# A fast matrix product over seven instead of six k pairs, with its recombination in one place

## The chip, the cores and the metric

One Trainium2 chip, one NeuronCore. The metric is the time on the device in microseconds (us), median of three runs. TensorE multiplies (its records are PE, and PEld for the loading of its stationary operand), VectorE (DVE) and ScalarE (ACT) work on vectors, GpSimd (POOL) issues some DMAs, SyncE (SP) issues the loads of the weights.

## The reference, cut to what matters

A decoder layer on 256 tokens of width 4096: attention in four branches, then a layer that retrieves experts. Its last step is the product that the change touches:

```
coef = gates * take_along_axis(act, experts)
wmat = zeros((256, 4096)).at[rows, experts].add(coef)      # float32
h = h + wmat @ v                                          # v is 4096 x 4096, float32
```

## The kernel before

**Products of float32.** TensorE multiplies a reduced form of float32 (fp32r). For full accuracy the kernel splits each operand in a high part (hi, rounded by ScalarE) and a remainder (lo = raw - hi, by VectorE), and computes hi x hi + lo x hi + hi x lo: three matmuls of 128 x 128 by 128 x 512 for each block product.

**Chunks and the ring.** Weights come in chunks of two k tiles by 512 columns (512 KB, 128 x 1024 floats) into a ring of four slots. For each chunk: SyncE loads `w_raw`, ScalarE makes `w_hi` (`hi`, L1091), VectorE makes `w_lo` (`lo`, L1484), TensorE multiplies. ScalarE may overwrite a slot of `w_hi` when TensorE has used the chunk four before (`chunk_used`), so the conversions run up to three chunks ahead of TensorE. SyncE loads into a slot of `w_raw` as soon as VectorE has made its `w_lo`.

**The V product.** Rows of wmat are two halves h of 128 tokens, columns of v are eight groups of 512, k is 32 tiles of 128, taken as 16 k pairs. Groups 0 and 1 run plainly. Groups 2 to 7 run as three column pairs m = 1, 2, 3 (`for m in range(1, PAIRS)`, each engine has this loop, L1077, L1469, L2195). One step of it is one k pair: two chunks, s for the pair's first column group and s + 1 for its second. Both hold the same two k tiles. In a plain k pair that is two halves x two k tiles x two groups = 8 block products, 24 matmuls. `products` (L582) does one chunk, 12 matmuls. The text calls the two column groups of a column pair block 0 and block 1, and numbers chunks from the start of column pair 1, 32 to each.

**The fast k pairs** (`FAST`, L93: 0, 2, 4, 6, 8, 10) treat these as 2 x 2 matrices of blocks and use Winograd's form of Strassen's method: 7 block products, 21 matmuls (`fast_products`, L993). It needs sums of the left blocks (`s_raw`, `s_hi`, `s_lo`, made once for all fast k pairs, in the last chunks of group 1: L2081, L1461, L2096) and sums of the right blocks per k pair: VectorE's `t_sums` (L2102) makes four blocks t, ScalarE `t_hi` (L1446), VectorE `t_lo` (L2120). t is held once: t_sums waits for the t_lo of the fast k pair before, t_hi for TensorE's last use of t (`t_used`). Four of the seven products are summed over all fast k pairs in the four banks of `side` (P1, P5, P6, P7), the others directly in the four banks of `acc`, one for each block and half, where the plain k pairs add too.

**The recombination** (`add_pure`, L2139): once per column pair VectorE adds P1, P1 + P6, P1 + P6 + P5 and so on into the rows of h, in nine instructions of 512 columns in four steps; behind five of them (L2147, L2149, L2150, L2154, L2158) VectorE waits for their own end through `then`, before the next may start. The last raises `pure_free`; TensorE waits for it before it starts the side banks of the next column pair (L1033). Before, steps 0 and 1 lie around the second conversion of k pair 13, steps 2 and 3 around that of k pair 14.

**The block additions** (`end_of_pair`, `add_block`, L2162): VectorE adds the `acc` banks of the column pair before to the rows of h, and each raises `block_free`. They stand in k pair 1 of the next column pair: both halves of block 0, then the conversion of chunk 34, then both halves of block 1, then that of chunk 35. TensorE waits for each bank before its first matmul into it (`wait_block`): in k pair 0, after P1's two hi matmuls and the nine matmuls from t, for block 0's first half, two matmuls later for block 1's, and before its last three for block 0's second half; in k pair 1 for block 1's second half.

**VectorE's order at the seam** between column pairs is its program's: conversions of k pair 15 (chunks 30 and 31), t_sums for the next column pair's k pair 0, conversions of chunk 32 and half of 33, t_lo, and then k pair 1 as above.

Of the kernel before, what the change touches and what calls it, by code (L numbers as in the profile page):

```python
# [69 lines left out]
CPG = KT // 2  # L70
# [19 lines left out]

CH_F = CH_V + 2 * CPG
PAIRS = GRP // 2
FAST = (0, 2, 4, 6, 8, 10)  # L93
NF = len(FAST)

NCMP = (S - 32) // 16 + 1
# [73 lines left out]
def fast_count(m, kp):  # L170

    return (m - 1) * NF + FAST.index(kp)

# [9 lines left out]
def build(nc, io):  # L183
# [175 lines left out]
    def sems(*names):  # L359
        return [nc.alloc_semaphore(n) for n in names]  # L360
# [41 lines left out]
    half_done, pure_free, block_free, last_stored = sems("half_done", "pure_free", "block_free", "last_stored")  # L402
# [20 lines left out]
    def pair_bank(i):  # L423

        return (GN_V + i) % 2
# [58 lines left out]
    with nc.Block() as block:  # L484
# [96 lines left out]
        def _(pe):  # L581
# [401 lines left out]
            def ring(slot):  # L983
                return [[w[:, slot, j * 512:(j + 1) * 512] for j in range(2)] for w in (w_hi, w_lo)]
# [8 lines left out]
            def fast_products(m, kp):  # L993

                n, a = fast_count(m, kp), CH_F + (m - 1) * 2 * CPG + 2 * kp
                first, last = kp == FAST[0], kp == FAST[-1]
                wa, wb = ring(a % RING), ring((a + 1) % RING)
                q = FAST.index(kp)
                s_tile = [(s_hi[:, i, q, :], s_lo[:, i, q, :]) for i in range(4)]
# [77 lines left out]
            for m in range(1, PAIRS):  # L1077
                for kp in range(CPG):
                    if kp in FAST:
                        fast_products(m, kp)  # L1080
# [5 lines left out]
        def _(act):  # L1086
# [4 lines left out]
            def hi(chunk, slot, width, m4):  # L1091

                act.wait_ge(raw_loaded[slot], raw_parts(m4) * 16)
                if not (isinstance(chunk, int) and chunk < RING):
                    act.wait_ge(chunk_used, chunk - (RING - 1))
                nc.scalar.activation(w_hi[:, slot, 0:width], w_raw[:, slot, 0:width], ACT.Copy).then_inc(hi_ready, 1)  # L1096
# [358 lines left out]
            def hi_half(chunk, slot):  # L1455

                act.wait_ge(raw_loaded[slot], raw_parts(chunk // RING) * 16)
                act.wait_ge(chunk_used, chunk - (RING - 1))
                nc.scalar.activation(w_hi[:, slot, 512:1024], w_raw[:, slot, 512:1024], ACT.Copy).then_inc(hi_ready, 1)
# [9 lines left out]
            for m in range(1, PAIRS):  # L1469
                for kp in range(CPG):  # L1470
                    s = CH_F + (m - 1) * 2 * CPG + 2 * kp
                    hi(s, s % RING, 1024, s // RING)
                    if kp in FAST:
                        hi_half(s + 1, (s + 1) % RING)
# [6 lines left out]
        def _(dve):  # L1481
            then = chain(dve, dve_chain)

            def lo(chunk, slot, width):  # L1484
                dve.wait_ge(hi_ready, chunk + 1)
                nc.vector.tensor_tensor(w_lo[:, slot, 0:width], w_raw[:, slot, 0:width],  # L1486
                                        w_hi[:, slot, 0:width].bitcast(F32), ALU.subtract).then_inc(lo_ready, 1)
# [306 lines left out]
            def add_rows(g, ch0, parity, rows=rows):  # L1794

                dve.wait_ge(chunk_used, g * CPG + (ch0 + CPG))
                for h in range(NT):
                    dst = rows[:, h, bass.ds(g * 512, 512)]
                    e = nc.vector.tensor_tensor(dst, acc[:, parity, h, :], dst, ALU.add)
                e.then_inc(bank_free[parity], 1)  # L1800
# [301 lines left out]
            def t_sums(m, kp):  # L2102

                n, s = fast_count(m, kp), CH_F + (m - 1) * 2 * CPG + 2 * kp
                a = s % RING
                if n == 0:
                    dve.wait_ge(s_lo_done, 4)
                else:
                    dve.wait_ge(t_lo_done, 2 * n)
                for i in range(2):  # L2110
                    dve.wait_ge(raw_loaded[a + i], raw_parts(s // RING) * 16)
                nc.vector.tensor_tensor(
                    t_raw[:, 0], w_raw[:, a + 1, :].rearrange("p (j n) -> p j n", j=2), w_raw[:, a:a + 2, 0:512],
                    ALU.subtract).then_inc(t_made, 1)
                dve.wait_ge(t_made, 2 * n + 1)
                then(nc.vector.tensor_tensor(t_raw[:, 1, 0], w_raw[:, a + 1, 512:1024], t_raw[:, 0, 0], ALU.subtract))
                nc.vector.tensor_tensor(t_raw[:, 1, 1], w_raw[:, a, 512:1024], t_raw[:, 1, 0], ALU.subtract)\
                    .then_inc(t_made, 1)

            def t_lo_part(m, kp):  # L2120

                n = fast_count(m, kp)
                for d in range(2):
                    dve.wait_ge(t_hi_done, 2 * n + d + 1)
                    nc.vector.tensor_tensor(flat(t_lo[:, d]), flat(t_raw[:, d]), flat(t_hi[:, d]).bitcast(F32),  # L2125
                                            ALU.subtract).then_inc(t_lo_done, 1)

            def lo_half(chunk, slot):

                dve.wait_ge(hi_ready, chunk + 1)  # L2130
                nc.vector.tensor_tensor(w_lo[:, slot, 512:1024], w_raw[:, slot, 512:1024],
                                        w_hi[:, slot, 512:1024].bitcast(F32), ALU.subtract).then_inc(lo_ready, 1)

            def block_rows_of(m, i, h):

                n = 2 * m + i
                return h_rows[:, h, n * 512:(n + 1) * 512]

            def add_pure(m, step):  # L2139

                u, v = sums[0][:], sums[1][:]
                p1, p5, p6, p7 = (side[:, i, :] for i in range(4))
                if step == 0:
                    dve.wait_ge(t_used, m * NF)
                    c = block_rows_of(m, 0, 0)
                    nc.vector.tensor_tensor(c, p1, c, ALU.add)
                    then(nc.vector.tensor_copy(u, p1))  # L2147
                elif step == 1:
                    then(nc.vector.tensor_tensor(u, p6, u, ALU.add))  # L2149
                    then(nc.vector.tensor_tensor(v, p5, u, ALU.add))  # L2150
                elif step == 2:
                    c = block_rows_of(m, 1, 0)
                    nc.vector.tensor_tensor(c, c, v, ALU.add)
                    then(nc.vector.tensor_tensor(u, p7, u, ALU.add))  # L2154
                else:
                    c = block_rows_of(m, 0, 1)
                    nc.vector.tensor_tensor(c, c, u, ALU.add)
                    then(nc.vector.tensor_tensor(v, p5, u, ALU.add))  # L2158
                    c = block_rows_of(m, 1, 1)
                    nc.vector.tensor_tensor(c, c, v, ALU.add).then_inc(pure_free, 1)  # L2160

            def add_block(m, i, h):  # L2162

                s = CH_F + m * 2 * CPG - 2 + i
                if h == 0:
                    dve.wait_ge(half_done, 2 * (m - 1) + i + 1)
                else:
                    dve.wait_ge(chunk_used, s + 1)
                c = block_rows_of(m, i, h)
                nc.vector.tensor_tensor(c, acc[:, pair_bank(i), h, :], c, ALU.add).then_inc(block_free, 1)  # L2170

            def end_of_pair(m, i):

                if m == 0:
                    if i == 1:
                        add_rows(1, CH_V, pair_bank(1), h_rows)
                else:
                    for h in range(NT):
                        add_block(m, i, h)

# [14 lines left out]
            for m in range(1, PAIRS):  # L2195
                for kp in range(CPG):
                    s = CH_F + (m - 1) * 2 * CPG + 2 * kp
                    if kp == 1:
                        end_of_pair(m - 1, 0)
                    lo(s, s % RING, 1024)  # L2200
                    if kp in FAST:
                        lo_half(s + 1, (s + 1) % RING)
                        t_lo_part(m, kp)
                        continue
                    if kp == 1:
                        end_of_pair(m - 1, 1)
                    if kp in (13, 14):
                        add_pure(m, 2 * (kp - 13))
                    lo(s + 1, (s + 1) % RING, 1024)
                    if kp + 1 in FAST:  # L2210
                        t_sums(m, kp + 1)
                    elif kp == CPG - 1 and m + 1 < PAIRS:
                        t_sums(m + 1, 0)
                    if kp in (13, 14):
                        add_pure(m, 2 * (kp - 13) + 1)
            for i in range(2):
                end_of_pair(PAIRS - 1, i)

# [152 lines left out]
```

## Time and profile before

| | |
|---|---|
| median of 3 runs | 1919.16 us (1918.83 to 1919.18) |
| profiled execution | 1918.33 us, span 1916.5 us |
| TensorE matmuls busy | 1912.1 us, 9230 instructions |
| VectorE busy | 1369.7 us (71%) |
| ScalarE busy | 962.2 us (50%) |
| granted clock | 1.000 |
| DMA | 412.70 MB, 215 GB/s |

Busy time is the union of an engine's instructions. Matmuls overlap in the records (the next starts before the one before it is recorded as ended), so a busy TensorE is one without gaps, and the distance between starts is what a matmul costs.

### The profile page before, as it was taken

The numbers are of one execution on the slowest core, as the hardware profiler recorded it, in microseconds if no ns is written. First come the engines' busy times: TensorE is split into PE (matmuls) and PEld (weight loads), VectorE is DVE, ScalarE is ACT, GpSimd is POOL, SyncE is SP. The second block draws the span as 40 slices with busy tenths as digits, with TensorE's granted clock in tenths as the row PEclk, the third lists the DMA queues.
The fourth block names the chain that finished last, engine by engine and source line by source line (L and its number), as shares of the span: only waits on it lengthen the run. The fifth ranks groups of instructions, "written<-read, shape, count | busy, mean of one in ns | idle before, by whom it ended". The sixth has DMA issues, their size and how long they took to land.

```text
span 1916.5 us, 26452 instructions
## 1 busy us (share of the span) xinstructions
PE 1912.1 (100%) x9230; PEld 1577.6 (82%) x9230; DVE 1369.7 (71%) x1999; ACT 962.2 (50%) x1184; POOL 36.3 (2%) x49
## 2 busy tenths in 40 slices
PE   9999999999999999999999999999999999999999
PEld 8888888888888888888888888888887788888887
DVE  6578775575557889655555555788879877789796
ACT  7653644445566556444444464444444454555453
POOL 0010010000000000000000000000000000000000
PEclk9999999999999999999999999999999999999999
DMA  9976667556655669877777776677766668666664
GB/s 324 352 221 166 168 176 195 170 156 168 182 183 176 185 194 295 290 225 239 236 229 236 215 227 221 229 213 216 218 210 190 186 200 306 209 215 212 206 221 152
DMA packets 198688, 412.70 MB, mean 215 GB/s; under 512 B 45776, under 2 KB 123984, under 8 KB 197936
## 3 DMA queue, kind: packets, MB, share of 16 engines
q1 hardware_dynamic: 173904, 369.35, 63.6%
q10 hardware_dynamic: 20976, 25.19, 3.9%
q0 software_dynamic: 3696, 16.65, 2.3%
q8 instruction: 73, 1.20, 0.3%
q14 instruction: 39, 0.32, 0.0%
HBM read 390.15 MB, written 20.97 MB: 215 GB/s over the span
## 4 chain that ended last, share of the span: by engine, by line
PE 100%; DVE 0%; issue 0%
PE acc L590 27%; PE acc L593 27%; PE acc L597 27%; PE acc L638 3%; PE acc L640 3%; PE acc L644 3%; PE acc L1066 1%; PE side L768 1%; PE side L979 1%; PE side L980 1%; PE side L981 1%; PE side L879 1%; PE acc L613 1%; PE acc L609 1%; PE acc L617 1%; PE acc L1071 0%
## 5 line engine op out<-in xcount | busy, mean ns | idle before, releaser
L1486 DVE TENSOR_TENSOR w_lo<-w_raw,w_hi 128x1024 fp32r<-128x1024 f32 (+1 forms) x662 | 802.9, 1215 | 496.7 <-ACT w_hi L1096 493.7
L1096 ACT ACTIVATE w_hi<-w_raw 128x1024 fp32r<-128x1024 f32 (+1 forms) x662 | 695.6, 1052 | 757.8 <-PE acc L597 655.3
L590 PE MATMUL acc<-w_hi,xt_hi 128*128 128x512 f32 x1484 | 402.0, 393 | 0.0
L593 PE MATMUL acc<-w_hi,xt_lo 128*128 128x512 f32 x1484 | 397.0, 389 | 0.0
L597 PE MATMUL acc<-w_lo,xt_hi 128*128 128x512 f32 x1484 | 396.9, 389 | 0.0
L593 PEld LDWEIGHTS acc<-w_hi,xt_lo 128*128 128x128 f32 x1484 | 278.6, 188 | 58.6
L597 PEld LDWEIGHTS acc<-w_lo,xt_hi 128*128 128x128 f32 x1484 | 278.6, 188 | 58.2
L590 PEld LDWEIGHTS acc<-w_hi,xt_hi 128*128 128x128 f32 x1484 | 275.7, 188 | 56.7 <-issue 1.8
L590 PE MATMUL acc<-w_hi,x_hi 128*128 128x512 f32 x640 | 175.1, 395 | 0.0
L593 PE MATMUL acc<-w_hi,x_lo 128*128 128x512 f32 x640 | 171.8, 390 | 0.0
L597 PE MATMUL acc<-w_lo,x_hi 128*128 128x512 f32 x640 | 171.2, 389 | 0.0
L593 PEld LDWEIGHTS acc<-w_hi,x_lo 128*128 128x128 f32 x640 | 120.1, 188 | 25.7
L597 PEld LDWEIGHTS acc<-w_lo,x_hi 128*128 128x128 f32 x640 | 120.2, 188 | 25.3
L590 PEld LDWEIGHTS acc<-w_hi,x_hi 128*128 128x128 f32 x640 | 117.2, 188 | 22.4
L1238 ACT ACTIVATE gate<-acc 128x512 f32<-128x512 f32 x64 | 34.8, 596 | 37.1 <-PE acc L597 35.5
L1453 ACT ACTIVATE t_hi<-t_raw 128x1024 fp32r<-128x1024 f32 x36 | 36.1, 1051 | 15.7 <-PE acc L981 15.7
L2125 DVE TENSOR_TENSOR t_lo<-t_raw,t_hi 128x1024 fp32r<-128x1024 f32 x36 | 42.4, 1219 | 0.8 <-ACT t_hi L1453 0.8
L590 PE MATMUL acc<-w_hi,zt_hi 128*128 128x512 f32 x128 | 34.5, 391 | 0.0
L597 PE MATMUL acc<-w_lo,zt_hi 128*128 128x512 f32 x128 | 34.2, 389 | 0.0
L593 PE MATMUL acc<-w_hi,zt_lo 128*128 128x512 f32 x128 | 34.2, 389 | 0.0
L1731 DVE TENSOR_TENSOR gate<-acc,gate 128x512 f32<-128x512 f32 x48 | 30.7, 682 | 0.0
L1180 ACT ACTIVATE probs<-probs,small 128x128 f32<-128x128 f32 (+2 forms) x44 | 18.3, 417 | 22.0 <-DVE small L1644 21.9
(330 smaller groups left out, 1756.7 us busy)
## 6 DMA issues: line engine op xcount, KB each, us to landing
w_raw<-in_stream SPq DMA_DIRECT2D x504, 512.0 KB, 4.2
w_raw<-in_w_in SPq DMA_DIRECT2D x16, 496.0 KB, 3.9
w_raw<-in_w_in SPq DMA_DIRECT2D x16, 480.0 KB, 4.1
w_raw<-in_w_in SPq DMA_DIRECT2D x16, 464.0 KB, 3.7
w_raw<-in_w_in SPq DMA_DIRECT2D x16, 448.0 KB, 3.9
w_raw<-in_w_in SPq DMA_DIRECT2D x16, 432.0 KB, 3.8
w_raw<-in_w_in SPq DMA_DIRECT2D x16, 416.0 KB, 4.1
w_raw<-in_w_in SPq DMA_DIRECT2D x16, 400.0 KB, 3.7
```

The lines of the kernel that those rows point to most:

```text
L590: pe.matmul(o[h], lhs(k0 + j, h)[0], wh[j], start=first and j == 0, stop=False)
L593: pe.matmul(o[h], lhs(k0 + j, h)[1], wh[j], start=False, stop=False)
L597: mm = pe.matmul(o[h], lhs(k0 + j, h)[0], wl[j], start=False, stop=last and j == 1)
L638: pe.matmul(o, lhs(k0 + j, h)[0], wh[j], start=first and j == 0, stop=False)
L640: pe.matmul(o, lhs(k0 + j, h)[1], wh[j], start=False, stop=False)
L644: mm = pe.matmul(o, lhs(k0 + j, h)[0], wl[j], start=False, stop=last and j == 1)
L1096: nc.scalar.activation(w_hi[:, slot, 0:width], w_raw[:, slot, 0:width], ACT.Copy).then_inc(hi_ready, 1)
L1238: e = nc.scalar.activation(gate[:, n % 2, h, :], acc[:, 1, h, :], ACT.Sigmoid)
L1453: nc.scalar.activation(flat(t_hi[:, d]), flat(t_raw[:, d]), ACT.Copy).then_inc(t_hi_done, 1)
L1486: nc.vector.tensor_tensor(w_lo[:, slot, 0:width], w_raw[:, slot, 0:width], w_hi[:, slot, 0:width].bitcast(F32), ALU.subtract).then_inc(lo_ ...
L1731: nc.vector.tensor_tensor(dst, acc[:, 0, h, :], gate[:, n % 2, h, :], ALU.mult)\
L2125: nc.vector.tensor_tensor(flat(t_lo[:, d]), flat(t_raw[:, d]), flat(t_hi[:, d]).bitcast(F32), ALU.subtract).then_inc(t_lo_done, 1)
```

## The change

The list of fast k pairs gets k pair 12. All four steps of the recombination move to k pair 15: two ahead of the conversion of its second chunk, two behind it, and ahead of t_sums for the next column pair. The block additions get a wait for `pure_free`. The S tiles grow with the list (`NF` is 7).

```diff
-FAST = (0, 2, 4, 6, 8, 10)
+FAST = (0, 2, 4, 6, 8, 10, 12)
 NF = len(FAST)
...
                 else:
+                    dve.wait_ge(pure_free, m)
                     for h in range(NT):
                         add_block(m, i, h)
...
                     if kp == 1:
                         end_of_pair(m - 1, 1)
-                    if kp in (13, 14):
-                        add_pure(m, 2 * (kp - 13))
+                    if kp == CPG - 1:
+                        add_pure(m, 0)
+                        add_pure(m, 1)
                     lo(s + 1, (s + 1) % RING, 1024)
+                    if kp == CPG - 1:
+                        add_pure(m, 2)
+                        add_pure(m, 3)
                     if kp + 1 in FAST:
                         t_sums(m, kp + 1)
                     elif kp == CPG - 1 and m + 1 < PAIRS:
                         t_sums(m + 1, 0)
-                    if kp in (13, 14):
-                        add_pure(m, 2 * (kp - 13) + 1)
```

## Rows read from the trace of the kernel before

**Rows 1.** The chain that ended last, share of the span by engine.
```profile
PE 100%; DVE 0%; issue 0%
```

**Rows 2.** Busy time by stage: stretch, length, each engine's busy us, PEclk, DMA share, GB/s.
```profile
1747.30:1830.30 83.00, 83.00 (x368) 68.73 (x367) 71.17 (x76) 42.58 (x44) 1.43 (x2) 1.00 0.67 215
1742.00:1754.00 12.00, 12.00 (x54) 9.93 (x54) 11.61 (x14) 7.27 (x9) 1.43 (x2) 1.00 0.72 243
1825.00:1837.00 12.00, 12.00 (x54) 9.95 (x53) 11.61 (x14) 7.32 (x9) 1.43 (x2) 1.00 0.70 239
1624.00:1658.00 34.00, 34.00 (x152) 28.15 (x151) 23.83 (x22) 16.20 (x15) 0.72 (x1) 1.00 0.70 205
```

**Rows 3.** TensorE's timeline: start, length; a fast k pair's first matmul, the next's.
```profile
1715.31 0.39 PE L1022 MATMUL side<-w_hi,xt_hi 128*128 128x512 f32 x1
...
1720.07 1.07 PE L590 MATMUL acc<-w_hi,xt_hi 128*128 128x512 f32 x4
```

**Rows 4.** ScalarE's timeline: w_hi of chunks 26 and 30, and t_hi.
```profile
1723.05 1.06 ACT L1096 ACTIVATE w_hi<-w_raw 128x1024 fp32r<-128x1024 f32 x1 [3.66 <-PE acc L597]
...
1733.93 1.06 ACT L1096 ACTIVATE w_hi<-w_raw 128x1024 fp32r<-128x1024 f32 x1 [1.66 <-PE acc L597]
...
1742.63 1.99 ACT L1453 ACTIVATE t_hi<-t_raw 128x1024 fp32r<-128x1024 f32 x2
```

**Rows 5.** VectorE's timeline in k pairs 13 and 14, with the recombination.
```profile
1724.14 1.23 DVE L1486 TENSOR_TENSOR w_lo<-w_raw,w_hi 128x1024 fp32r<-128x1024 f32 x1 [3.30 <-ACT w_hi L1096]
1725.29 0.68 DVE L2146 TENSOR_TENSOR h_rows<-side,h_rows 128x512 f32<-128x512 f32 x1
1725.88 0.68 DVE L2147 COPY sums<-side 128x512 f32<-128x512 f32 x1
...
1733.52 0.69 DVE L2157 TENSOR_TENSOR h_rows<-h_rows,sums 128x512 f32<-128x512 f32 x1
1734.12 0.68 DVE L2158 TENSOR_TENSOR sums<-side,sums 128x512 f32<-128x512 f32 x1
1734.84 0.69 DVE L2160 TENSOR_TENSOR h_rows<-h_rows,sums 128x512 f32<-128x512 f32 x1
1735.45 1.22 DVE L1486 TENSOR_TENSOR w_lo<-w_raw,w_hi 128x1024 fp32r<-128x1024 f32 x1
```

**Rows 6.** VectorE's timeline at the seam between column pairs 1 and 2.
```profile
1738.88 1.22 DVE L2112 TENSOR_TENSOR t_raw<-w_raw 128x1024 f32<-128x1024 f32 x1
...
1741.47 1.22 DVE L1486 TENSOR_TENSOR w_lo<-w_raw,w_hi 128x1024 fp32r<-128x1024 f32 x1
...
1743.71 2.36 DVE L2125 TENSOR_TENSOR t_lo<-t_raw,t_hi 128x1024 fp32r<-128x1024 f32 x2 [0.26 <-ACT t_hi L1453]
1745.98 1.28 DVE L2170 TENSOR_TENSOR h_rows<-acc,h_rows 128x512 f32<-128x512 f32 x2
1747.18 1.22 DVE L1486 TENSOR_TENSOR w_lo<-w_raw,w_hi 128x1024 fp32r<-128x1024 f32 x1
1748.32 1.28 DVE L2170 TENSOR_TENSOR h_rows<-acc,h_rows 128x512 f32<-128x512 f32 x2
...
1754.37 0.68 DVE L2131 TENSOR_TENSOR w_lo<-w_raw,w_hi 128x512 fp32r<-128x512 f32 x1
1754.97 1.22 DVE L2125 TENSOR_TENSOR t_lo<-t_raw,t_hi 128x1024 fp32r<-128x1024 f32 x1
```

**Rows 7.** TensorE's timeline in column pair 2's k pair 0, matmuls and a weight load.
```profile
1747.50 0.19 PEld L979 LDWEIGHTS side<-t_hi,s_hi 128*128 128x128 f32 x1
...
1747.72 0.39 PE L979 MATMUL side<-t_hi,s_hi 128*128 128x512 f32 x1
...
1750.22 0.39 PE L1022 MATMUL acc<-w_hi,s_hi 128*128 128x512 f32 x1
```

**Rows 8.** Timeline of the kernel's start.
```profile
0.88 0.33 DVE L2181 MEMSET warm<- 128x320 uint32 x1 [0.88 <-PEq L2359]
...
1.26 5.66 PE L624 MATMUL side<-warm 128*128 128x512 bf16 x13 [1.26 <-DVE warm L2181]
```

## The prediction

> **What bounds the kernel now.** I read the chain of waits first: all of it is TensorE [rows 1]. Then I read busy time by stage. In the stretch of one column pair of the V product TensorE is busy for all of 83.00 us and VectorE for 71.17, but in the 12 us around the seam between two pairs VectorE is busy for 11.61 of 12.00, and both seams read alike [rows 2]. So the kernel is TensorE's list of matmuls from end to end, and VectorE has room on average and none at the seams. The change adds to VectorE's work exactly before a seam, so the third view is the order of instructions there, engine by engine.
>
> A matmul's record is 0.39 us long, but that is no price: they overlap. From the first matmul of a fast k pair to the first of the next k pair are 4.76 us for 21 matmuls, so one costs 0.2267 us [rows 3]. A plain chunk of 12 is 2.72 us, a plain k pair of 24 is 5.44 us.
>
> **The change, part by part.**
>
> *Seventh fast k pair.* In each of three column pairs k pair 12 has 21 matmuls instead of 24. That removes 9 x 0.2267 = 2.04 us from an engine that never waits. It is exact as long as nothing waits.
>
> *More conversion work in k pair 12.* ACT gets two t conversions for half a chunk's, VectorE gets t_sums (2.59 us), a half conversion for a whole one and two t_lo. The kernel already runs fast, plain, fast, plain for k pairs 0 to 11 with TensorE at 83.00 of 83.00, so one more period of the same pattern costs nothing; its cover is the ring, as now. VectorE is through with it in time for k pair 15: behind the last fast k pair and the four conversions after it, it now idles 3.30 us until ACT gives it the next w_hi [rows 5], and that idle time now moves to just before chunk 30.
>
> *Longer S tiles* (7 x 128 instead of 6 x 128 columns in four sums, two conversions, two remainders) lie in the last chunks of the group before. There VectorE works for 23.83 of 34 us with the six-part tiles, and TensorE for all 34 [rows 2]. Even a sixth more of all that work would leave 6 us idle: 0.
>
> *The recombination moves.* Nine VectorE instructions per column pair used to lie in four gaps of k pairs 13 and 14, in which VectorE waited for ACT anyway. Now they stand in k pair 15, four before the conversion of chunk 31 and five after, and t_sums of the next column pair, the conversions of its chunks 32 and 33 and t_lo stand behind them. This is the part that decides, so I work out VectorE's queue at the seam from column pair 1 to 2, in the times of the profile before (in the changed kernel all is 0.68 us earlier per column pair, on every engine alike). Chunks are numbered from the start of column pair 1, so 30 and 31 are its last two and 32 and 33 the first of column pair 2.
>
> The steps from start to start, from rows: ACT's conversion to w_lo 1.09 [rows 4, 5]; w_lo to the next 1.15, recombination with no wait 0.59 or 0.60, with the chain's wait for its own end 0.72, the last one to what follows 0.61 [rows 5]; t_sums 2.59, half conversion to t_lo 0.60, both t_lo 2.27, two block additions 1.20, w_lo to the addition behind it 1.14, one addition 0.68 long [rows 6]; one t_lo 1.22 long [rows 6].
>
> ACT starts w_hi of chunk 30 at 1733.93, which TensorE sets and the change does not touch [rows 4]. Then:
> w_lo 30 starts 1735.02; recombination L2146 1736.17, L2147 1736.76, L2149 1737.48, L2150 1738.20; w_lo 31 1738.92 (its w_hi has long been there); L2153 1740.07, L2154 1740.67, L2157 1741.39, L2158 1741.99, L2160 1742.71; t_sums 1743.32; w_lo 32 1745.91; half of 33 1747.05; t_lo 1747.65, its first half done at 1748.87, both issued by 1749.92; additions of block 0 at 1749.92; w_lo 34 at 1751.12; addition of block 1, first half, 1752.26, done at 1752.94.
> Before, t_sums started at 1738.88, t_lo at 1743.71, the additions at 1745.98 and 1748.32 [rows 6]: the block additions are 3.94 us later.
>
> ACT is no limit in this: its two t_hi take 1.0 us each [rows 4] and wait for t_sums, whose halves end near 1744.5 and 1746.0, so they end near 1745.6 and 1747.1, before VectorE comes to t_lo.
>
> Against that, TensorE's needs. In the first fast k pair of a column pair the products from t are the third to eleventh matmul, due at 1747.72; then come the two matmuls into the first bank of block 0, then at 1750.22 those into block 1's [rows 7]. Each bank has to be emptied by its block addition first.
> - t products: due 1747.72, t_lo there at 1748.87. First stall, about 1.3 us.
> - block 0's bank: with nine matmuls (2.04 us) between, due about 1751.06, emptied at 1749.92 + 0.68 = 1750.60. No stall.
> - block 1's bank: due at 1751.5, emptied at 1752.94. Second stall, about 1.6 us. The addition is held up by w_lo 34, which stands ahead of it in the queue.
> TensorE so starts that matmul at 1752.94 plus a restart. The trace of before has hardly a restart of TensorE. From the end of VectorE's memset at the start (0.88 + 0.33 = 1.21) to the first matmul at 1.26 are 0.05 us [rows 8]; with a whole weight load of 0.19 in the open, 0.24 or 0.25 [rows 7]. I take 0.15, between the two. The seam costs 1752.94 + 0.15 - 1750.22 = 2.87 us (2.77 to 2.97).
>
> What stands behind the seam recovers. VectorE's chain goes on: addition 1752.86, w_lo 35 1753.46, t_sums 1754.60, w_lo 36 1757.19, half of 37 1758.33, t_lo 1758.93, its first half done at 1760.15. TensorE has 8 matmuls after 1753.09 and a plain k pair, so k pair 2 starts at 1754.90 + 5.44 = 1760.34 and its t products, which are last there, at 1762.38. That leaves 2.2 us.
>
> *How often.* A seam of this kind lies behind column pairs 1 and 2, not behind 3: there no t_sums follows and no product waits, and the last additions wait for the last matmuls as now. At the entry to column pair 1 no recombination stands in the queue. So two seams, 5.74 us (5.54 to 5.94).
>
> *The new wait* for pure_free ahead of the block additions stands on the engine that raised it, over 6 us earlier: 0 to 0.05. Nothing is queued behind it longer than behind the additions themselves. The bank waits of TensorE for pure_free (the side banks) are met at 1743.4, before 1747.27.
>
> **Sum**: -2.04 + 5.74 = +3.70 us (+3.50 to +3.90). The profiled execution took 1918.33 us with a span of 1916.5, the median of the runs is 1919.16, 0.83 more; the forecast is 1918.33 + 3.70 = 1922.03 for the profile and 1919.16 + 3.70 = 1922.86 for the median, 0.193% above.
>
> **The rivals.**
> *Only the cut shows* (-2.04: 1917.1). VectorE idles 12 us of 83 [rows 2], TensorE never waits today, and the recombination could lie in that idle time. The point from which it decides: the addition of block 1 out by 1750.1, 2.9 us earlier than I have it. Against: the idle time of the last plain k pairs lies before w_hi 30 and can't be saved up. By the Trainium skill, "Perfetto Trace Analysis", section "Identifying the Most-Contended Engine", one improves a kernel through the engine with the highest occupancy, here TensorE; that rule would give this rival. Chance 0.06.
> *One stall instead of two* (1.3 per seam: -2.04 + 2.6 = +0.56, 1919.7). It needs the addition of block 1 some 1.5 us earlier, as when VectorE's start-to-start times behind each other are shorter than where they were measured. All are from back-to-back rows, so it is unlikely. Chance 0.06.
> *TensorE loses its clock at a seam.* The granted clock is 1.00 in all stages [rows 2]. But the first 13 matmuls of the kernel, after idle time, take 5.66 us, 0.43 us for each 512 columns, which is the 1.2 GHz level, against 0.227 later [rows 3, 8]. If each seam's stalls brought such a stretch back, 13 x 0.20 = 2.6 us each: +3.70 + 5.2 = +8.9, 1928.1. The stalls are 1.3 and 1.6 us with eleven matmuls between, so I give 0.04. The Trainium skill, "TensorE: Matmul & The Clock Gate", section "Why this matters for your kernels", warns of idle gaps between bursts of matmuls that send the clock back to the half rate; by it this rival would be the price of a longer stall, and the trace of before has no gap to test it on.
> *A further wait behind the seam* (a late load for t_sums, or more of the chain than I see, with the 2.2 us of margin gone): +1 us each, 1924.9. Chance 0.04.
>
> **How the numbers follow.** Forecast 0.80. About 0.2% (3.84 us) is what can be told from no change, and the forecast of +3.70 stands just inside it: I give 0.42 of that case to more than 3.84 (0.34) and the rest (0.46) to less. With the last two rivals slower is 0.42; same gets 0.46 + 0.06 + 0.06, less 0.02 for something that I don't see on the fast side: 0.56; faster 0.02. The range goes from 1921.0 to 1925.0: the bounds of the sum, some tenths of error for each chain of some fifteen steps, and the further wait.
>
> **What would show it.** Right: TensorE's busy time falls and its idle time at two seams is no longer 0: waits of its weight loads for VectorE's t_lo (L2125) and for h_rows (L2170), 1.3 and 1.6 us, two of each, and none at k pair 12. VectorE without a gap from w_lo 30 to k pair 3. The 83.0 us between the first fast matmuls of column pairs 1 and 2 become 83.0 - 0.68 + 2.87 = 85.2. Wrong: no idle time on TensorE at the seams, a stall elsewhere, or matmuls at 0.43 us each behind one.

## The result and the profile after

The changed kernel takes 1922.87 us (median of 18 runs, 1922.49 to 1923.42) against 1918.97 us (18 runs, 1918.37 to 1919.36): +3.90 us, ratio 1.0021, 95% interval 1.0014 to 1.0027. The interval lies wholly above 1, so the kernel is slower, by 0.203%. On which side of the 0.2% that the prediction named it lies the interval doesn't say. Its profiled execution took 1922.52 us with a span of 1920.7 us.

First TensorE's busy time and VectorE's, from the page after:

```profile
PE 1911.1 (100%) x9221; PEld 1575.1 (82%) x9221; DVE 1383.2 (72%) x2014; ACT 968.2 (50%) x1190; POOL 36.3 (2%) x49
```

TensorE has nine matmuls less and is busy 1.0 us less, with a span that is 4.2 us longer. (The other 1.0 us of the cut of 2.04 doesn't show in busy time: at each of the four stalls the last record stands to its full 0.39 us instead of being overlapped after 0.23, and the matmuls behind a stall start further apart.) The waits of TensorE in the whole trace after (waiter, releaser, total us, times, longest) say where it now stands still; the last two are the kernel's start:

```profile
PE acc L1022 <- DVE h_rows L2170: 2.6, 2, 1.3
PE side L979 <- DVE t_lo L2125: 2.3, 2, 1.1
PE side L624 <- DVE warm L2182: 1.3, 1, 1.3
PE acc L609 <- ACT w_hi L1096: 0.3, 1, 0.3
```

Two waits, each twice: for t_lo and for the block addition. By stage, with the columns of [rows 2], column pair 2 and the two seams:

```profile
1746.84:1832.12 85.28, 82.85 (x364) 67.98 (x363) 75.10 (x81) 44.15 (x47) 1.43 (x2) 1.00 0.64 210
1742.00:1754.00 12.00, 9.57 (x42) 7.31 (x41) 11.90 (x15) 4.39 (x6) 1.30 (x2) 1.00 0.46 155
1827.00:1839.00 12.00, 9.54 (x42) 7.32 (x41) 11.90 (x15) 4.60 (x5) 1.01 (x2) 1.00 0.46 158
```

VectorE works for 11.90 of the 12 us, and now TensorE is the one that waits, by the records 2.4 us per seam. Records of matmuls reach over the next one's start, so what a seam costs is read from starts: 2.99 us, as shown below. These are TensorE's, around the first seam:

```profile
1746.84 0.39 PE L1022 MATMUL side<-w_hi,xt_hi 128*128 128x512 f32 x1
1747.07 0.39 PE L1023 MATMUL side<-w_hi,xt_lo 128*128 128x512 f32 x1
1748.60 0.47 PE L979 MATMUL side<-t_hi,s_hi 128*128 128x512 f32 x1 [1.14 <-DVE t_lo L2125]
1748.90 0.39 PE L980 MATMUL side<-t_hi,s_lo 128*128 128x512 f32 x1
...
1750.75 0.39 PE L1022 MATMUL acc<-w_hi,xt_hi 128*128 128x512 f32 x1
1750.98 0.39 PE L1023 MATMUL acc<-w_hi,xt_lo 128*128 128x512 f32 x1
1752.66 0.47 PE L1022 MATMUL acc<-w_hi,s_hi 128*128 128x512 f32 x1 [1.29 <-DVE h_rows L2170]
1752.97 0.40 PE L1023 MATMUL acc<-w_hi,s_lo 128*128 128x512 f32 x1
...
1754.59 1.08 PE L590 MATMUL acc<-w_hi,xt_hi 128*128 128x512 f32 x4
```

The fast k pair takes 1754.59 - 1746.84 = 7.75 us instead of 4.76 [rows 3]: 2.99 us lost. By starts, less the 0.23 us that a matmul takes, the stalls are 1748.60 - 1747.07 - 0.23 = 1.30 us and 1752.66 - 1750.98 - 0.23 = 1.45 us. And these are VectorE's starts, where [rows 5, 6] had the recombination in gaps and the seam 3.9 us earlier:

```profile
1734.60 1.23 DVE L1486 TENSOR_TENSOR w_lo<-w_raw,w_hi 128x1024 fp32r<-128x1024 f32 x1 [3.30 <-ACT w_hi L1096]
1735.74 0.68 DVE L2146 TENSOR_TENSOR h_rows<-side,h_rows 128x512 f32<-128x512 f32 x1
...
1738.51 1.22 DVE L1486 TENSOR_TENSOR w_lo<-w_raw,w_hi 128x1024 fp32r<-128x1024 f32 x1
1739.65 0.69 DVE L2153 TENSOR_TENSOR h_rows<-h_rows,sums 128x512 f32<-128x512 f32 x1
...
1742.91 1.22 DVE L2112 TENSOR_TENSOR t_raw<-w_raw 128x1024 f32<-128x1024 f32 x1
...
1747.23 2.36 DVE L2125 TENSOR_TENSOR t_lo<-t_raw,t_hi 128x1024 fp32r<-128x1024 f32 x2
1749.50 1.28 DVE L2170 TENSOR_TENSOR h_rows<-acc,h_rows 128x512 f32<-128x512 f32 x2
1750.70 1.22 DVE L1486 TENSOR_TENSOR w_lo<-w_raw,w_hi 128x1024 fp32r<-128x1024 f32 x1
1751.83 1.28 DVE L2170 TENSOR_TENSOR h_rows<-acc,h_rows 128x512 f32<-128x512 f32 x2
```

A bracket would show idle time. There is none behind the first line, nor in the lines left out: for 18 us VectorE never waits for another engine. TensorE's column pairs start at 1664.57, 1746.84 and 1832.12: 82.27 us for the first (82.96 before, less 0.68), then 85.28. The third is as long, 85.25 to the end of its last matmul's 0.23 us. So the sum over the three is 252.80 against 248.88 before, +3.92, and the medians give +3.90.

### The profile page after: what moved, and what is told of

Read it like the earlier page. It is cut to its first block, busy times and chain, and to the rows that moved or that the text cites. A ratio compares the mean times of both kernels' runs of the same rounds, so it can differ in the third digit from the quotient of the medians.

```text
span 1920.7 us, 26467 instructions
## 1 busy us (share of the span) xinstructions
PE 1911.1 (100%) x9221; PEld 1575.1 (82%) x9221; DVE 1383.2 (72%) x2014; ACT 968.2 (50%) x1190; POOL 36.3 (2%) x49
## 4 chain that ended last, share of the span: by engine, by line
PE 97%; DVE 2%; DMA 0%; issue 0%; ACT 0%; SPq 0%; ACTq 0%
PE acc L590 26%; PE acc L593 26%; PE acc L597 26%; PE acc L638 3%; PE acc L640 3%; PE acc L644 3%; PE side L768 1%; PE side L980 1%; PE side L981 1%; PE side L979 1%; PE side L879 1%; PE acc L1022 0%; PE acc L1028 0%; PE acc L609 0%; DVE w_lo L1486 0%; PE acc L613 0%
## 5 line engine op out<-in xcount | busy, mean ns | idle before, releaser
L590 PE MATMUL acc<-w_hi,xt_hi 128*128 128x512 f32 x1460 | 395.6, 393 | 0.0
L593 PE MATMUL acc<-w_hi,xt_lo 128*128 128x512 f32 x1460 | 390.6, 389 | 0.0
L597 PE MATMUL acc<-w_lo,xt_hi 128*128 128x512 f32 x1460 | 390.5, 389 | 0.0
L593 PEld LDWEIGHTS acc<-w_hi,xt_lo 128*128 128x128 f32 x1460 | 274.0, 188 | 57.7
L597 PEld LDWEIGHTS acc<-w_lo,xt_hi 128*128 128x128 f32 x1460 | 274.0, 188 | 57.4
L590 PEld LDWEIGHTS acc<-w_hi,xt_hi 128*128 128x128 f32 x1460 | 271.1, 188 | 55.9 <-issue 1.8
L1453 ACT ACTIVATE t_hi<-t_raw 128x1024 fp32r<-128x1024 f32 x42 | 42.8, 1056 | 24.5 <-PE acc L981 19.3
L2125 DVE TENSOR_TENSOR t_lo<-t_raw,t_hi 128x1024 fp32r<-128x1024 f32 x42 | 49.4, 1218 | 0.0
```

The costliest lines, as they stand in the source:

```text
L590: pe.matmul(o[h], lhs(k0 + j, h)[0], wh[j], start=first and j == 0, stop=False)
L593: pe.matmul(o[h], lhs(k0 + j, h)[1], wh[j], start=False, stop=False)
L597: mm = pe.matmul(o[h], lhs(k0 + j, h)[0], wl[j], start=False, stop=last and j == 1)
L1453: nc.scalar.activation(flat(t_hi[:, d]), flat(t_raw[:, d]), ACT.Copy).then_inc(t_hi_done, 1)
```

## The experiments

Each is timed against the kernel before on the same chip; there it took 1918.91 us in the first four and 1918.94 in the last two.

**The move alone.** Six fast k pairs, everything else as changed.

```diff
-FAST = (0, 2, 4, 6, 8, 10, 12)
+FAST = (0, 2, 4, 6, 8, 10)
```

> The move alone: six fast k pairs as before, the recombination in k pair 15 as in the changed kernel, and the new wait. Theory A (VectorE's queue at the two seams): the trace of the changed kernel shows its k pair 1 starting 2.99 us late behind a seam (1754.59 against 1746.84 + 4.76), so 2 x 2.99 = +5.98 us against the kernel before, 1924.9 us, with the same two stalls (1.1 and 1.3 us by the records) at each seam. Theory B (part of the loss is the seventh fast k pair itself, by more work on VectorE in k pair 12 or longer S tiles): less than +5.5 us.

1924.86 us, +5.95, ratio 1.0030 (1.0019 to 1.0042). TensorE's waits at the seams are those of the changed kernel, to the tenth:

```profile
PE acc L1022 <- DVE h_rows L2170: 2.6, 2, 1.3
PE side L979 <- DVE t_lo L2125: 2.3, 2, 1.1
```

The changed kernel's +3.90 lies 2.05 us below this, which is the cut of 2.04. So the whole loss is the move's, and theory B's price for the seventh fast k pair is not there.

**Seven fast k pairs, the recombination in VectorE's idle time.** In the changed kernel:

```diff
-                    if kp == CPG - 1:
-                        add_pure(m, 0)
-                        add_pure(m, 1)
                     lo(s + 1, (s + 1) % RING, 1024)
-                    if kp == CPG - 1:
-                        add_pure(m, 2)
-                        add_pure(m, 3)
+                    if kp == CPG - 2:
+                        for step in range(4):
+                            add_pure(m, step)
```

> Seven fast k pairs, all four steps of the recombination right behind the second conversion of k pair 14, where the changed kernel's VectorE idles 3.30 us. Theory A: nine instructions of 5.97 us start near 1731.7 (times of the kernel before), end by 1737.8, the conversions of chunks 30 and 31 follow at 1737.8 and 1738.9, t_sums at 1740.1, t_lo at 1744.4, the addition of block 1 done at 1749.7, before TensorE's matmul is due at 1750.22: no stall, -2.04 us, 1916.9 us. Theory B: the seventh fast k pair costs something of its own, so less than the 2.04 us comes, down to none.

1916.98 us, -1.93, ratio 0.9989 (0.9980 to 0.9998): the fastest of all, and the cut of 2.04 comes through but for 0.1. VectorE's lines at the same place:

```profile
1729.24 2.36 DVE L1486 TENSOR_TENSOR w_lo<-w_raw,w_hi 128x1024 fp32r<-128x1024 f32 x2 [0.59 <-ACT w_hi L1096]
1731.51 0.68 DVE L2146 TENSOR_TENSOR h_rows<-side,h_rows 128x512 f32<-128x512 f32 x1
...
1737.54 2.35 DVE L1486 TENSOR_TENSOR w_lo<-w_raw,w_hi 128x1024 fp32r<-128x1024 f32 x2
1739.81 1.22 DVE L2112 TENSOR_TENSOR t_raw<-w_raw 128x1024 f32<-128x1024 f32 x1
```

The 3.30 us of idle time ahead of chunk 30 is gone, filled with the recombination, and t_sums starts 3.4 us earlier than in the changed kernel (1739.81 against 1742.91, with this trace 0.31 us later at the first line). TensorE waits for nothing at the seams. The conversion of chunk 30 starts 2.6 us later than ACT would allow (1737.54 against 1733.81 + 1.09), and TensorE doesn't need it sooner.

**Half of it in the idle time.** In the changed kernel:

```diff
-                    if kp == CPG - 1:
+                    lo(s + 1, (s + 1) % RING, 1024)
+                    if kp == CPG - 2:
                         add_pure(m, 0)
                         add_pure(m, 1)
-                    lo(s + 1, (s + 1) % RING, 1024)
                     if kp == CPG - 1:
                         add_pure(m, 2)
                         add_pure(m, 3)
```

> Seven fast k pairs, steps 0 and 1 of the recombination behind the second conversion of k pair 14, steps 2 and 3 behind that of k pair 15. Theory A: four instructions lie in idle time, five (3.24 us) at the seam. t_sums near 1742.1, t_lo's first half done at 1747.7 (stall 0.1), the addition of block 1 done at 1751.75, its matmul at 1751.90 instead of 1750.22: with the slow start behind a stall 1.8 us per seam, -2.04 + 3.6 = +1.5 us, 1920.5 us. If the first stall alone decided: -1.8 us.

1920.59 us, +1.68, ratio 1.0008 (0.9999 to 1.0017). The wait for t_lo is gone from the list, the other stays, twice:

```profile
PE acc L1022 <- DVE h_rows L2170: 2.6, 2, 1.3
```

VectorE's additions of block 1 and the matmul that waits for the first of them:

```profile
1751.08 1.28 DVE L2170 TENSOR_TENSOR h_rows<-acc,h_rows 128x512 f32<-128x512 f32 x2
...
1751.91 0.47 PE L1022 MATMUL acc<-w_hi,s_hi 128*128 128x512 f32 x1 [1.32 <-DVE h_rows L2170]
```

The column pair starts at 1747.28 here, so this matmul, behind 13 others, is due at 1747.28 + 2.95 = 1750.23. The addition is out at 1751.08 + 0.68 = 1751.76, and the matmul starts 0.15 us behind it, 1.68 us late; k pair 1 is 1.77 us late. So the second stall doesn't come from the first: it is the block addition's being late.

**The block additions ahead of the conversion.** The changed kernel, with the only difference that in k pair 1 both blocks' additions stand before the conversion of chunk 34:

```diff
                     if kp == 1:
                         end_of_pair(m - 1, 0)
+                        if m > 1:
+                            end_of_pair(m - 1, 1)
                     lo(s, s % RING, 1024)
...
-                    if kp == 1:
+                    if kp == 1 and m == 1:
                         end_of_pair(m - 1, 1)
```

> The changed kernel with the additions of block 1 ahead of the conversion of chunk 34 instead of behind it. Theory A: t_lo and the first stall stay (1.3 us), the addition of block 1 is done 1.14 us earlier, 1751.8 in the times of the kernel before, so the second stall falls to 0.4 us: some 1.85 us per seam, -2.04 + 3.7 = +1.7 us, 1920.6 us. A theory in which the wait for t_lo is all: no change against the changed kernel, +3.9 us.

1920.59 us, +1.68, ratio 1.0008 (0.9999 to 1.0017). Here the first stall stays and the second shrinks:

```profile
PE side L979 <- DVE t_lo L2125: 2.3, 2, 1.1
...
PE acc L1022 <- DVE h_rows L2170: 0.3, 2, 0.2
```

The four additions now stand together, and the same matmul starts 1.73 us late (1751.38 against 1746.70 + 2.95), k pair 1 1.84 us late:

```profile
1749.36 2.48 DVE L2170 TENSOR_TENSOR h_rows<-acc,h_rows 128x512 f32<-128x512 f32 x4
...
1751.38 0.47 PE L1022 MATMUL acc<-w_hi,s_hi 128*128 128x512 f32 x1 [0.19 <-DVE h_rows L2170]
```

Each of these two runs brings 2.2 us of the changed kernel's 5.9. A theory in which the wait for t_lo is all of it falls with both: here that wait is unchanged and 2.2 us come back, and in the run before it is gone and most of the loss stays. But the two stalls aren't two prices either. In the changed kernel, the half in idle time and this one, the matmul into block 1's bank is 2.87, 1.68 and 1.73 us late, and the seam costs 2.99, 1.77 and 1.84: the time at which VectorE is through with block 1's first addition, and some 0.1 us. TensorE waits for t_lo within time that it would have waited for that addition anyway. That is argued from these three; no run has t_lo early and leaves the addition where it was.

**A long stall.** In the changed kernel, eight more copies ahead of the recombination:

```diff
                     dve.wait_ge(t_used, m * NF)
+                    for _ in range(8):
+                        then(nc.vector.tensor_copy(u, p1))
```

> The changed kernel with eight further copies of 512 columns from a side bank (each waits for its own end, 0.72 us) ahead of the recombination in k pair 15: 5.76 us more in VectorE's queue at each seam, so the first stall grows to some 7 us. Theory A (only the queue counts): +3.9 + 2 x 5.76 = +15.4 us against the kernel before, 1934.4 us, with matmuls 0.227 to 0.24 us apart behind the stall. Theory C (TensorE loses its clock in such a stall): matmuls 0.43 us apart for a while behind it, by the kernel's start some 13 of them, 2.6 us more per seam: +20.6 us, 1939.6 us.

1938.86 us (4 runs), +19.92, ratio 1.0107 (1.0092 to 1.0123), between the two expectations. It is near theory C's 1939.6 by luck, as the parts below show. TensorE around the first seam:

```profile
1748.63 0.50 PE L1022 MATMUL side<-w_hi,xt_hi 128*128 128x512 f32 x1 [1.15 <-DVE h_rows L2162]
1748.97 0.40 PE L1023 MATMUL side<-w_hi,xt_lo 128*128 128x512 f32 x1
1754.18 0.77 PE L979 MATMUL side<-t_hi,s_hi 128*128 128x512 f32 x1 [4.81 <-DVE t_lo L2125]
1754.74 0.63 PE L980 MATMUL side<-t_hi,s_lo 128*128 128x512 f32 x1
1755.17 0.63 PE L981 MATMUL side<-t_lo,s_hi 128*128 128x512 f32 x1
...
1757.22 0.39 PE L980 MATMUL side<-t_hi,s_lo 128*128 128x512 f32 x1
1757.46 0.40 PE L981 MATMUL side<-t_lo,s_hi 128*128 128x512 f32 x1
```

There is one more wait here, 1.15 us for `pure_free` (L2162) ahead of the side banks, as the copies hold up the recombination too. And the clock does fall: matmuls behind the stall start 0.43 us apart, the 1.2 GHz level, and 0.23 to 0.24 apart seven matmuls later. The granted clock by stage (the third column from the end):

```profile
1746.00:1750.00 4.00, 2.21 (x9) 1.19 (x7) 3.90 (x6) 0.20 (x1) 0.00 (x0) 1.00 0.45 131
1750.00:1754.00 4.00, 0.00 (x0) 0.00 (x0) 3.97 (x6) 3.67 (x4) 0.00 (x0) 0.54 0.13 16
1754.00:1758.00 4.00, 3.82 (x11) 3.03 (x11) 4.00 (x6) 0.14 (x1) 0.71 (x1) 0.61 0.63 253
1758.00:1762.00 4.00, 4.00 (x19) 3.14 (x18) 3.93 (x6) 2.50 (x3) 0.72 (x1) 1.00 0.99 340
```

But it costs nearly nothing, since the slow matmuls lie in the time in which block 1's addition would have been waited for anyway. That addition's first half is out at 1758.10 at the first seam and at 1848.46 + 0.68 = 1849.14 at the second, and the matmuls that wait for it start here:

```profile
1758.24 0.47 PE L1022 MATMUL acc<-w_hi,s_hi 128*128 128x512 f32 x1
...
1848.46 1.28 DVE L2172 TENSOR_TENSOR h_rows<-acc,h_rows 128x512 f32<-128x512 f32 x2
...
1849.70 0.40 PE L1022 MATMUL acc<-w_hi,s_hi 128*128 128x512 f32 x1
```

The first starts 0.14 us behind the addition, so the addition still sets it; the second 0.56 us behind, so there the slow stretch does. With column pairs due 82.28 us apart as above, the first seam costs 8.76 us, the queue alone would make it 2.99 + 5.76 = 8.75; the second costs 9.11, 0.36 more. What theory A missed lies in column pair 3. There VectorE ends the copies so late that the last block additions end 3.77 us behind TensorE's last matmul slot instead of 0.89 (+2.9), and w_lo of chunk 31 comes late (+0.7). In all 8.76 + 9.11 + 3.6 - 2.04 = 19.4, against 19.8 by the spans; the other 0.4 us stays open.

**The new wait alone.** The kernel before, with `dve.wait_ge(pure_free, m)` ahead of the block additions.

> The kernel before with only the new wait of VectorE for pure_free ahead of the block additions. Theory A: the semaphore was raised over 6 us earlier, and VectorE's sequencer runs ahead: 0.0 us, 1919.0 us. A theory in which the wait takes part in the stall at the seam: up to +0.1 us per seam and no idle time of TensorE in the profile of this kernel, as its margins are 1 us and more.

1918.82 us, -0.12, ratio 0.9999 (0.9990 to 1.0008), and no wait of TensorE at a seam: it costs nothing that can be measured. In the changed kernel itself the additions start 2.27 us behind t_lo and 1.13 behind w_lo of chunk 34, against 2.27 and 1.14 in [rows 6], where there was no such wait.

## Why the prediction was right

*The cut* was right in size. 2.04 us was forecast; the first column pair is 0.69 us shorter, and with the recombination in idle time the kernel is 1.93 us faster.

*The queue at the seam* was right by place, kind and time. In times of the kernel before (the changed kernel's plus 0.43 here, as its second column pair starts at 1746.84 instead of 1747.27) t_sums stands at 1743.34 (forecast 1743.32), t_lo at 1747.66 (1747.65), the block additions at 1749.93 and 1752.26 (1749.92 and 1752.26). VectorE's back-to-back rows carried over to an order in which they had never stood.

*The two stalls* and their count: two seams, both waits at each, none at k pair 12 and none behind the seam, as said. The forecast priced a seam at the second stall's end alone, and the third and fourth runs bear that out. The price was 2.87 (bounds 2.77 to 2.97) and measured 2.97 to 3.00, so at or just past the upper bound. The term that was too small is the restart. From VectorE's end at 1751.83 + 0.68 = 1752.51 to the first matmul at 1752.66 are 0.15 us, as taken. But the next starts 0.31 us later instead of 0.227, and the following ones 0.23 to 0.24 apart: the eight matmuls up to k pair 1 take 1.93 us instead of 1.81. These 0.12 per seam are the 0.2 us between +3.70 and +3.90. They put the median at 0.203%, where the prediction had 0.193% and gave 0.42 to slower by more than 0.2% and 0.56 to less; the interval of 0.14% to 0.27% doesn't decide between the two. One sign came in another form: the profile puts the waits for t_lo and h_rows down to the matmuls (1.1 and 1.3 us), and the longer idle time of the weight loads (1.5 and 1.7 us) to "issue".

*The S tiles, the conversions of k pair 12 and the wait* cost nothing, shown by the run with the recombination in idle time, which has all three, and by the wait alone.

*The rivals.* "Only the cut shows" failed here, and is what the kernel does once the recombination lies elsewhere. "One stall instead of two" did not come. The third and fourth runs are near it, with block 1's addition some 1.2 us earlier instead of 1.5 and a seam at 1.8 us instead of 1.3. The clock held at 1.00 through both seams of the changed kernel, with stalls of 1.30 and 1.45 us by starts. It fell in the run with the long stall. There the trace agrees with the Trainium skill, "TensorE: Matmul & The Clock Gate", section "Why this matters for your kernels", that an idle gap sends the clock back to half rate: 1.00 before, 0.54 within the 4.81 us, seven to nine matmuls at 0.43 us behind it. "A further wait behind the seam" did not come.

The rule of the Trainium skill, "Perfetto Trace Analysis", section "Identifying the Most-Contended Engine", would have given the wrong sign here: TensorE was the engine with the highest occupancy, it got less to do, and the kernel became slower. By the average VectorE had some 28% to spare; in the 12 us that count it had 3%.

## What to carry to other kernels

Work on an engine that is idle for more than a quarter of its time is free only where the idle time is. Before moving a block of it, write down the engine's queue from there to the next thing that another engine waits for, with start-to-start times of back-to-back instructions, and hold it against the other engine's due times one by one; here that gave every start within 0.02 us. Then price the last hand-over, not each wait: an earlier wait can lie inside it. Here the idle time lay where VectorE waited for ACT's w_hi, which waited for TensorE to free its slot. The recombination cost nothing right ahead of such a wait, and 5.95 us behind it.

## What the runs showed of the hardware

A wait of TensorE costs more than its gap: 0.15 us from VectorE's recorded end to the first matmul, 0.08 more on the second, and some 0.01 on each of the next few.

A seam's slow clock can be hidden by the next wait. The long stall had seven and nine matmuls at 1.2 GHz, worth some 1.4 and 1.8 us against the 2.15 us that the same nine matmuls took behind the short stall, and of these 3.2 us only about 0.4 show in the seams' lengths.
